# RWKV preparation and inversion: key norms summed token-major, sigmoids of both directions together, triangular inversion by predicated copies without GpSimd

## The chip, the cores and the metric

One core of one Trainium2 chip runs the whole program. The metric is the device time in microseconds (us) of one execution, and the median of several runs counts. Engines are called PE (TensorE), DVE (VectorE), ACT (ScalarE), POOL (GpSimd) and SP (SyncE, which here only issues transfers).

## The reference

The program computes two trunk layers over 384 tokens (128 of a prompt, 256 latent ones, width 1024). Each layer is a SwiGLU half step, a token mixer and another SwiGLU half step, each with adaptive modulation and a layer norm behind it. The mixer has three branches: differential attention, gated linear attention (GLA) and RWKV-7. The change touches the RWKV branch (and a clamp inside the GLA stage):

```python
kk = heads(k * lp['rw_k_k'])
kk = kk / jnp.maximum(jnp.sqrt(jnp.sum(jnp.square(kk), -1, keepdims=True)), 1e-12)
for d, pd in enumerate((dir_f, dir_b)):
    w_raw = lp['rw_w0'][d] + jnp.tanh(wd) @ lp['rw_w_up'][d]
    decay = jnp.exp(-jnp.exp(-jax.nn.softplus(-w_raw) - 0.5))
    a = jax.nn.sigmoid(lp['rw_a0'][d] + ad @ lp['rw_a_up'][d])
    kd = heads(k * (1.0 + (a - 1.0) * lp['rw_k_a']))
    ...
    y, s_fin = rwkv7_scan(*seq, s0[:, d])
```

With four heads of 64 and chunks of 64 tokens, `rwkv7_scan` is done chunk-wise: prefix sums of the log decay (a scan along the tokens), decayed keys and receptances, 64x64 products of them, the inverse X of a unit triangular 64x64 matrix per chunk, head and direction, and then products with that inverse.

## The kernel before

A layer is one block of straight code per engine; the stages are separated by `meet()`, a meeting of PE, DVE, ACT and POOL. SP streams the weights, 1 MB at a time, into a ring of six slots, and a slot is refilled when PE releases it (`used`). While attention, GLA and RWKV run, the ring is full and nothing is fetched. Feature-major tiles have features on the 128 partitions and tokens along the row: `WIN` is the stretch of 385 columns that holds three groups of 128 tokens, and a `wide` tile is two such rows (770 columns, four heads).

**GLA tail** (DVE `gla()`, lines 2063 to 2087). Behind the last GLA output DVE scales the keys (L2068), squares them (L2070), and works on the GLA outputs. In between it takes the sums of squares, which PE makes with a 128x128 block of ones so that each sum stands on all 64 partitions of its head (L1114, 2 x 385 columns), and clamps them (L2079). ACT takes the root of the 770 columns (L1670).

**Preparation** (`rwkv()` of each engine). DVE inverts the 770 roots (L2091) and normalises the keys (L2092). Then, for direction 0 and after it direction 1: PE's low-rank products `lora(d)` (L1104), four sigmoids on ACT into `sw` (decay) and `sa` (rate) (L1663, L1665), two scans on DVE (L2101) and a subtraction (L2103), three exponentials on ACT (L1680, L1683, L1684), the keys on DVE (L2108, L2111), four products on DVE (L2114 to L2118) and three small copies (L2121). `sw`, `sa` and `cs` exist once, so `rates(1)` waits for `decay_used`, at the end of direction 0. POOL makes `be = sa * kk` (L2343) and `rkd = r * kn` (L2347) for each direction; the second `rkd` waits for PE's bonus product of the first (`bonus_mm`), and the bonus product (L1135) is what DVE copies last (L2125) before the meeting. PE does `products(0)` and `products(1)` (L1083) behind `decay_used` of direction 0.

**Units** (`rwkv_units()`, lines 1139 on for PE, 2127 on for DVE). Six (group, direction) products are masked into SBUF by DVE, `masked(n)` (L2133 and L2135, two of each per n); ACT copies the raw products into `am` (L1691), and `first(g)` masks them (L2143). The inverse is made level by level for three groups: X0 is the inverse so far, X1 its transpose, and at each of the levels v = 1 to 5 the off-diagonal half L of `am` gives X0 <- X0 - X0 L X0. PE forms L X0 (L1168) for three groups, ACT copies it (L1698), PE forms X0 L X0 (L1179) and its transpose (L1186), and DVE subtracts them from the banks (L2163, L2168). POOL adds the identity to both halves of each group (L2357, six times 128x512) and masks `am` for each level into `off` (L2361); PE waits for `off_ready` before each L1168. Behind it come token-major copies, the solves (L1209) with a negation on DVE (L2181), and the carries.

Of the kernel before, what the change touches and what calls it, by code (L numbers as in the profile page):

```python
# [9 lines left out]
I32 = mybir.dt.int32  # L10
# [96 lines left out]
def shape_constants():  # L107
# [102 lines left out]
def trunk_kernel(nc, x_in, c_in, consts, weights, w_ad, par_in, ln_in, row_in, bgate_in, rw_state_in, gla_state_in,  # L210
                 kc_in, vc_in, first_ada, b_first, y_out, rw_out, gla_out, k_out, v_out, dumps=None):
    with ExitStack() as ctx:
# [35 lines left out]
        arena, arena_r = with_rounded("arena", [P, 23660])  # L248
# [87 lines left out]
        g_kl = put(2 * TOK).rearrange("p (d t) -> p d t", d=2)  # L336
        g_o = put(2 * GROUPS * GLA_W).rearrange("p (d g n) -> p d g n", d=2, g=GROUPS)
        g_st = lnrow[:, 0, :].rearrange("p (d s n) -> p d s n", d=2, s=2)
# [22 lines left out]
        put.at = 0  # L361
        sw, sa, cs = wide(), wide(), wide()
        assert put.at <= ffn_mark
# [23 lines left out]
        off = by_head()  # L387
# [37 lines left out]
        att_sum = small[:, 28:52].rearrange("p (u c) -> p u c", c=2)  # L425
        diff_ss = small[:, 52:64]
# [107 lines left out]
        norm_root = sem("norm_root")  # L534
        kk_ready = sem("kk_ready")
# [9 lines left out]
        decay_used = sem("decay_used")  # L545
        bonus_in = sem("bonus_in")
# [5 lines left out]
        xz_first = sem("xz_first")  # L552
        xz_ready = sem("xz_ready")
        off_ready = sem("off_ready")
# [218 lines left out]
        def layer(l, last):  # L773
            with nc.Block() as block:
# [29 lines left out]
                def _(pe):  # L804
# [293 lines left out]
                    def rwkv():  # L1098
# [14 lines left out]
                        for i in range(2):  # L1113
                            mm = pe.matmul(ps[4 + i][:, 0:WPAD - 2], con("ones_blk"), kk[:, i, WIN], start=True, stop=True)  # L1114
# [9 lines left out]
                        lora(1)  # L1124

# [13 lines left out]
                    def rwkv_units():  # L1139
# [285 lines left out]
                def _(sc):  # L1425
# [230 lines left out]
                    def rwkv():  # L1656
                        def rates(d):
                            sc.wait_ge(lora_mm, d + 1)
                            if d == 1:
                                sc.wait_ge(decay_used, 1)  # L1660
                                sc.wait_ge(rate_kk, 1)
                            for i in range(2):
                                sc.activation(sw[:, i, WIN], ps[4 * d + 2 * i][:, 0:WPAD - 2], ACT.Sigmoid,  # L1663
                                              bias=w0[:, d, i:i + 1])
                                ins = sc.activation(sa[:, i, WIN], ps[4 * d + 2 * i + 1][:, 0:WPAD - 2], ACT.Sigmoid,  # L1665
# [4 lines left out]
                        sc.activation(pp[:, :, WIN], pp[:, :, WIN], ACT.Sqrt).then_inc(norm_root, 1)  # L1670
# [4 lines left out]
                        ins.then_inc(values_out, 1)  # L1675
                        for d in range(2):
                            if d == 1:
                                rates(1)
                            sc.wait_ge(cum_ready, d + 1)
# [104 lines left out]
                def _(ve):  # L1784
# [175 lines left out]
                    def gla():  # L1960
# [128 lines left out]
                    def rwkv():  # L2089
                        ve.wait_ge(norm_root, 1)  # L2090
                        own.link(ve.reciprocal(pp[:, :, WIN], pp[:, :, WIN]))  # L2091
                        ve.tensor_tensor(kk[:, :, WIN], kn[:, :, WIN], pp[:, :, WIN], ALU.mult).then_inc(kk_ready, 1)  # L2092
                        ve.wait_ge(kk_ready, 1)
                        k_, r_ = psh[:, 4:6, WIN], psh[:, 2:4, WIN]
                        for d in range(2):
                            ve.wait_ge(rates_ready, d + 1)
                            for i in range(2):
                                a, b, keep = cs[:, i, WIN], sw[:, i, WIN], rw_keep[:, d, WIN]
# [4 lines left out]
                            ve.tensor_tensor(sw[:, :, WIN], cs[:, :, WIN], sw[:, :, WIN], ALU.subtract).then_inc(cum_ready, 1)  # L2103

                            if d == 1:
# [410 lines left out]
```

## Time and profile before

| | |
|---|---|
| median of three runs | 2249.46 us (2248.36 to 2250.56) |
| profiled execution | 2254.03 us |
| its span, first to last instruction | 2252.2 us |
| mean granted TensorE clock | 0.917 of full speed |
| busy PE / DVE / ACT / POOL | 1960.7 / 1091.1 / 703.3 / 120.1 us |
| layer 2: GLA tail and preparation | 1719.8 to 1765.8 us |
| layer 2: units up to the first X0 L X0 | 1765.8 to 1784.2 us |
| layer 2: rest of the inversion | 1784.2 to 1821.6 us |

Times inside a trace are from the start of the span. Layer 1 passes through the same stages 1109.3 us earlier. A row of the chain or the timeline gives start and duration; "x32" means that many instructions in a row, and an instruction that follows another without a wait overlaps it by its latency, so that the distance of two starts is less than a duration. A multiplication of full 32-bit numbers stands as two PE records. Where a program's row names `arena`, it is the one large SBUF tensor out of which nearly all tiles are cut.

### The profile page before, as it was taken

To read this page: it belongs to the slowest core of one execution; us is meant where nothing else is said; L and a number is where in the kernel's file an instruction comes from. 1 tells how busy PE (TensorE), PEld (TensorE's weight loads), DVE (VectorE), ACT (ScalarE), POOL (GpSimd) and SP (SyncE) were. 2 spreads that over 40 slices of the span, in tenths; PEclk is the share of its full clock that TensorE was granted. 3 is DMA by queue.
4 is the path that set the end of the run, shared out by engine and by line. 5 is a ranking of instruction groups with operands and counts; after the bars stand their busy time and mean duration, and the time that the engine had idled before them with its cause. 6 is when DMAs were issued, how large, how long until landed. Compare 5 with 4: busy or idle time off the path is not lost. (4 is left out here: it accounts for less than half of the span.)

```text
span 2252.2 us, 36981 instructions
## 1 busy us (share of the span) xinstructions
PE 1960.7 (87%) x15584; PEld 1727.6 (77%) x15584; DVE 1091.1 (48%) x1655; ACT 703.3 (31%) x1155; POOL 120.1 (5%) x104
## 2 busy tenths in 40 slices
PE   5999998997549779999969999999964688899995
PEld 3899995985439659999849999869843686699994
DVE  0434336526674663343453343454287647634345
ACT  1422222335432332222232222133354223422221
POOL 1000001000031010000010000010000400100000
PEclk9899998998669989999969999989976799899998
DMA  7533336331000173333463333453300003633320
GB/s 321 219 131 130 116 127 261 113 125 53 13 1 4 60 280 112 131 125 118 152 241 133 129 130 116 156 214 132 122 23 8 2 4 112 257 120 130 130 93 28
DMA packets 40402, 274.39 MB, mean 122 GB/s; under 512 B 4740, under 2 KB 6548, under 8 KB 8288
## 3 DMA queue, kind: packets, MB, share of 16 engines
q1 hardware_dynamic: 35280, 255.34, 32.1%
q0 software_dynamic: 2400, 11.50, 1.3%
q10 hardware_dynamic: 2608, 5.88, 0.7%
q8 instruction: 90, 1.47, 0.3%
q14 instruction: 24, 0.20, 0.0%
HBM read 269.29 MB, written 3.41 MB: 121 GB/s over the span
## 5 line engine op out<-in xcount | busy, mean ns | idle before, releaser
L1791 DVE TENSOR_TENSOR ring_r<-ring,arena_r 128x1024 fp32r<-128x1024 f32 x280 | 327.6, 1221 | 657.7 <-ACT arena_r L1433 657.5
L842 PE MATMUL bank<-arena_r,ring_r 128*128 128x384 f32 x1728 | 586.9, 340 | 0.0
L838 PE MATMUL bank<-arena_r 128*128 128x384 f32 (+1 forms) x1504 | 519.0, 345 | 18.7 <-DVE arena_r L1811 12.9
L841 PE MATMUL bank<-arena_r 128*128 128x384 f32 x1408 | 475.7, 338 | 0.0
L842 PEld LDWEIGHTS bank<-arena_r,ring_r 128*128 128x128 f32 x1728 | 327.2, 189 | 0.0
L838 PEld LDWEIGHTS bank<-arena_r 128*128 128x128 f32 x1504 | 286.6, 191 | 30.8 <-DVE ring_r L1791 18.2
L884 PE MATMUL bank<-arena_r 128*128 128x512 f32 x1056 | 300.7, 393 | 0.0
L1433 ACT ACTIVATE arena_r<-ring 128x1024 fp32r<-128x1024 f32 x280 | 276.7, 1050 | 42.0 <-PE bank L842 30.4
L1472 ACT ACTIVATE arena<-bank 128x384 f32<-128x384 f32 x88 | 43.3, 492 | 756.9 <-PE bank L842 756.9
L841 PEld LDWEIGHTS bank<-arena_r 128*128 128x128 f32 x1408 | 265.7, 189 | 4.7 <-issue 1.0
L884 PEld LDWEIGHTS bank<-arena_r 128*128 128x128 f32 x1056 | 197.3, 188 | 38.5
L884 PE MATMUL bank<-ring_r,arena_r 128*128 128x512 f32 x528 | 164.4, 392 | 0.0
L666 PE MATMUL bank<-ring,silu_c 128*32 128x256 f32 x1152 | 101.3, 498 | 50.3 <-DVE arena L1847 29.2
L1791 DVE TENSOR_TENSOR ring_r<-ring,lnrow_r 128x1024 fp32r<-128x1024 f32 x60 | 73.4, 1225 | 147.3 <-ACT lnrow_r L1433 147.2
L884 PEld LDWEIGHTS bank<-ring_r,arena_r 128*128 128x128 f32 x528 | 99.1, 188 | 23.0
L838 PE MATMUL bank<-arena_r,lnrow_r 128*128 128x384 f32 x320 | 111.5, 349 | 4.0 <-DVE ring_r L1791 4.0
L666 PEld LDWEIGHTS bank<-ring,silu_c 128*32 128x32 f32 x1152 | 39.3, 135 | 97.4 <-DVE arena L1847 31.6
L841 PE MATMUL bank<-arena_r,lnrow_r 128*128 128x384 f32 x320 | 107.9, 337 | 0.0
L1433 ACT ACTIVATE lnrow_r<-ring 128x1024 fp32r<-128x1024 f32 x60 | 63.3, 1059 | 142.5 <-PE bank L842 142.5
L2324 POOL TENSOR_TENSOR x<-x,lnrow 128x1024 f32<-128x1024 f32 x12 | 28.2, 2348 | 1359.5 <-DVE x L1870 1359.5
L841 PE MATMUL bank<-ring_r,arena_r 128*128 128x512 f32 (+1 forms) x240 | 89.8, 374 | 0.0
L838 PEld LDWEIGHTS bank<-arena_r,lnrow_r 128*128 128x128 f32 x320 | 60.7, 190 | 5.9 <-DVE ring_r L1791 5.4
(295 smaller groups left out, 2372.1 us busy)
## 6 DMA issues: line engine op xcount, KB each, us to landing
ring<-weights SPq DMA_DIRECT2D x230, 1024.0 KB, 4.9
ring<-first_ada SPq DMA_DIRECT2D x12, 1024.0 KB, 13.4
lnrow<-ln_in POOLq DMA_DIRECT2D x6, 1024.0 KB, 6.5
const<-consts ACTq DMA_DIRECT2D x1, 2403.0 KB, 12.5
x<-x_in ACTq DMA_DIRECT2D x1, 1536.0 KB, 18.3
y_out<-x SPq DMA_DIRECT2D x3, 512.0 KB, 2.6
rows<-row_in POOLq DMA_DIRECT2D x2, 736.0 KB, 14.2
par<-par_in POOLq DMA_DIRECT2D x2, 626.0 KB, 8.8
```

The source lines that it names most:

```text
L666: mm = pe.matmul(ps[q // 2][rows_at, (q % 2) * 256:(q % 2) * 256 + 256], silu_c[:, 2 * (k % 2):2 * (k % 2) + 32], ring_tile(n0 + q)[:, k, ...
L838: mm = pe.matmul(out, w_h, h_h, start=start, stop=False, skip_group_check=True)
L841: pe.matmul(out, w_h, h_l, start=False, stop=False, skip_group_check=True)
L842: return pe.matmul(out, w_l, h_h, start=False, stop=stop, skip_group_check=True)
L884: mm = pe.matmul(ps[2 + 2 * g + n][:, :], a, w[:, n * 512:n * 512 + 512], start=(first and a is a_hi and w is hi), stop=(last and a is a_l ...
L1433: sc.activation(place, unit_of(FIRST[stretch], u), ACT.Copy).then_inc(w_rounded, 1)
L1472: sc.activation(sgt[:, b, :], ps[0][:, 0:TOK], ACT.Silu).then_inc(silu_done, 1)
L1791: ve.tensor_tensor(low_unit(FIRST[stretch], u), raw, place.bitcast(F32), ALU.subtract).then_inc(w_ready, 1)
L2324: po.tensor_tensor(x[:, g, :], x[:, g, :], lnrow[:, 1, :], ALU.add).then_inc(x_ready, 1)
```

## The change

1. **Norms.** PE multiplies each 128x128 tile of squares (now the stationary operand) by two columns of the block of ones, into 12 columns of one bank: the sums stand with tokens on partitions. Clamp, root and inverse act on 128x12. Twelve products of the inverse (one column stepped by zero into 64) with the identity then spread them back over the 64 partitions of each head, into banks 0 and 1, behind `lora(1)`; DVE multiplies out of PSUM.
2. **Order.** `sw`, `sa` and `cs` exist for both directions (`sw[1]` and `sa[1]` in parts of `psh` that are dead by then; `g_o` moves to the arena's start and the arena grows by 44 columns). ACT does both sets of sigmoids, then all exponentials. DVE does scan 0, kk, keys 0, scan 1, products 0, keys 1, products 1. The first product waits for the first exponential alone.
3. **Inversion.** ACT writes minus the identity into all of X0 and X1 ahead of time (two copies of 128x1536, behind the exponentials of direction 0), so the tiles hold minus the inverse. DVE puts the masked values in with `copy_predicated`, in place of the multiplications by a mask and the subtractions; PE uses the whole `am` and the mask of the level decides which of the results are written. POOL's part of the units, `off` and six semaphore waits go. The negation L2181 becomes a plain copy.

```diff
 # constants
-    first[:, 0, d] = -1.0 * half(cs, ct, 1, 1 - d)
-    first[:, 1, d] = -1.0 * half(cs, ct, 1, d)
+    first[:, 0, d] = half(cs, ct, 1, 1 - d)
+    first[:, 1, d] = half(cs, ct, 1, d)
 # tiles
-sw, sa, cs = wide(), wide(), wide()
+sw, sa, cs = (wide(), psh[:, 6:8, :]), (wide(), psh[:, 8:10, :]), (wide(), wide())
+kk_norm = small[:, 28:40]
 # PE, rwkv
-for i in range(2):
-    mm = pe.matmul(ps[4 + i][:, 0:WPAD - 2], con("ones_blk"), kk[:, i, WIN], start=True, stop=True)
+for g in range(GROUPS):
+    for i in range(2):
+        mm = pe.matmul(ps[4][:, 4 * g + 2 * i:4 * g + 2 * i + 2], kk[:, i, pcol(g):pcol(g) + P],
+                       con("ones_blk")[:, 0::64], start=True, stop=True)
 mm.then_inc(norm_mm, 1)
...
 lora(1)
+pe.wait_ge(norm_inv, 1)
+pe.wait_ge(rates_ready, 1)
+for i in range(2):
+    for g in range(GROUPS):
+        o, width = pcol(g) - 1, P + 1 if g == 0 else P
+        for par in range(2):
+            n = 4 * g + 2 * i + par
+            mm = pe.matmul(ps[i][64 * par:64 * par + 64, o:o + width],
+                           kk_norm[:, n:n + 1].to_broadcast([P, 64]), const[:, 0:width],
+                           start=True, stop=True)
+mm.then_inc(norm_wide, 1)
 # PE, units
-pe.wait_ge(off_ready, n + 1)
 if v == 1:
-    pe.wait_ge(xz_ready, 2 * g + 1)
-    if g == 1:
-        pe.wait_ge(prod_ready, 5)
-    else:
-        pe.wait_ge(am_ready, 2 if g == 0 else 3)
+    pe.wait_ge(prod_ready, (3, 5, 6)[g])
+    pe.wait_ge(am_ready, (2, 2, 3)[g])
...
-        mm = pe.matmul(ps[LX_BANK[g]][k, o:o + 64], off[k, g, d, h, :], xz[k, 0, g, d, h, :],
+        mm = pe.matmul(ps[LX_BANK[g]][k, o:o + 64], am[k, g, d, h, :], xz[k, 0, g, d, h, :],
                        start=True, stop=True)
...
-    pe.wait_ge(xz_ready, 2 * g + 2)
+    pe.wait_ge(xz_ready, g + 1)
 # ACT, rwkv
     sc.wait_ge(lora_mm, d + 1)
-    if d == 1:
-        sc.wait_ge(decay_used, 1)
-        sc.wait_ge(rate_kk, 1)
...
-sc.activation(pp[:, :, WIN], pp[:, :, WIN], ACT.Sqrt).then_inc(norm_root, 1)
+sc.activation(kk_norm, kk_norm, ACT.Sqrt).then_inc(norm_root, 1)
...
+rates(1)
 for d in range(2):
-    if d == 1:
-        rates(1)
     sc.wait_ge(cum_ready, d + 1)
-    own.link(sc.activation(sw[:, :, WIN], sw[:, :, WIN], ACT.Exp, scale=DECAY))
-    if d == 0:
-        sc.wait_ge(kk_ready, 1)
-    own.link(sc.activation(pp[:, :, WIN], cs[:, :, WIN], ACT.Exp, scale=DECAY))
-    sc.activation(cs[:, :, WIN], cs[:, :, WIN], ACT.Exp, scale=-DECAY).then_inc(decay_exp, 1)
+    ins = sc.activation(sw[d][:, :, WIN], sw[d][:, :, WIN], ACT.Exp, scale=DECAY)
+    ins.then_inc(decay_first, 1)
+    if d == 1:
+        sc.wait_ge(decay_used, 1)
+    own.link(sc.activation(pp[:, :, WIN], cs[d][:, :, WIN], ACT.Exp, scale=DECAY))
+    sc.activation(cs[d][:, :, WIN], cs[d][:, :, WIN], ACT.Exp, scale=-DECAY).then_inc(decay_exp, 1)
+    if d == 0:
+        for s in range(2):
+            sc.activation(xz[:, s, :, :, :, :].rearrange("p g d h n -> p (g d h) n"),
+                          ident64.unsqueeze(1).to_broadcast([P, 2 * GROUPS * HEADS, CHUNK]), ACT.Copy,
+                          scale=-1.0).then_inc(xz_filled, 1)
 # DVE, gla
-for i in range(2):
-    ins = ve.tensor_scalar(pp[:, i, WIN], ps[4 + i][:, 0:WPAD - 2], 1e-24, None, ALU.max)
-ins.then_inc(norm_sq, 1)
+ve.tensor_scalar(kk_norm, ps[4][:, 0:12], 1e-24, None, ALU.max).then_inc(norm_sq, 1)
 # DVE, rwkv: cumulate(d) is L2096 to L2103, keys(d) L2107 to L2112, decayed(d) L2114 to L2122
-own.link(ve.reciprocal(pp[:, :, WIN], pp[:, :, WIN]))
-ve.tensor_tensor(kk[:, :, WIN], kn[:, :, WIN], pp[:, :, WIN], ALU.mult).then_inc(kk_ready, 1)
+    def decayed(d):
+        ve.wait_ge(decay_first, d + 1)
+        own.step(ve.tensor_tensor(kr[:, 0, d, :, WIN], kk[:, :, WIN], sw[d][:, :, WIN], ALU.mult))
         ve.wait_ge(decay_exp, d + 1)
...
+ve.reciprocal(kk_norm, kk_norm).then_inc(norm_inv, 1)
+cumulate(0)
+ve.wait_ge(norm_wide, 1)
+for i in range(2):
+    ins = ve.tensor_tensor(kk[:, i, WIN], kn[:, i, WIN], ps[i][:, 0:WPAD - 2], ALU.mult)
+ins.then_inc(kk_ready, 1)
+ve.wait_ge(kk_ready, 1)
+keys(0)
+cumulate(1)
+decayed(0)
+ve.wait_ge(decay_used, 1)
+ve.wait_ge(bonus_in, 1)
+keys(1)
+decayed(1)
 # DVE, units
-        ins = ve.tensor_tensor(xz[:, 0, g, d, par::2, :], got[:, :, 0, :],
-                               rw_first[:, 0, d, :].unsqueeze(1).to_broadcast([P, 2, CHUNK]), ALU.mult)
+        ins = ve.copy_predicated(
+            xz[:, 0, g, d, par::2, :],
+            rw_first[:, 0, d, :].bitcast(I32).unsqueeze(1).to_broadcast([P, 2, CHUNK]), got[:, :, 0, :])
...
-    ve.tensor_tensor(xz[:, 1, g, :, :, :], am[:, g, :, :, :],
-                     rw_first[:, 1, :, :].unsqueeze(2).to_broadcast(wide), ALU.mult).then_inc(xz_first, 1)
+    ve.copy_predicated(xz[:, 1, g, :, :, :],
+                       rw_first[:, 1, :, :].bitcast(I32).unsqueeze(2).to_broadcast(wide),
+                       am[:, g, :, :, :]).then_inc(xz_ready, 1)
+ve.wait_ge(xz_filled, 2)
 masked(0)
...
-if v == 1:
-    ve.wait_ge(xz_ready, 2 * g + 2)
-else:
-    ve.wait_ge(inv_ready, n - GROUPS + 1)
 ve.wait_ge(xlx0_mm, n + 1)
-ins = ve.tensor_tensor(xz[:, 0, g, :, :, :].rearrange("p d h n -> p (d h n)"),
-                       xz[:, 0, g, :, :, :].rearrange("p d h n -> p (d h n)"),
-                       ps[XLX_BANK[g]][:, :], ALU.subtract)
+ins = ve.copy_predicated(
+    xz[:, 0, g, :, :, :], rw_halves[:, ::-1, v - 1, :].bitcast(I32).unsqueeze(2).to_broadcast(wide),
+    ps[XLX_BANK[g]][:, :].rearrange("p (d h n) -> p d h n", d=2, h=HEADS))
...
-    ve.tensor_scalar(to[:, g, :, :, :].rearrange("p d h n -> p (d h n)"), ps[bank][:, :], -1.0, None,
-                     ALU.mult).then_inc(uw_out, 1)
+    ve.tensor_copy(to[:, g, :, :, :].rearrange("p d h n -> p (d h n)"),
+                   ps[bank][:, :]).then_inc(uw_out, 1)
 # POOL: be reads sa[d]; rwkv_units (L2349 to L2363) is gone
```

## Rows read from the trace of the kernel before

**Rows 1.** The page: busy time of the engines.

```profile
PE 1960.7 (87%) x15584; PEld 1727.6 (77%) x15584; DVE 1091.1 (48%) x1655; ACT 703.3 (31%) x1155; POOL 120.1 (5%) x104
```

**Rows 2.** Windows: length, busy PE, PEld, DVE, ACT, POOL, granted clock, DMA share, GB/s.

```profile
1719.80:1765.81 46.01, 14.62 (x114) 10.62 (x114) 40.06 (x44) 20.13 (x26) 9.19 (x6) 0.65 0.03 9
1765.81:1784.20 18.39, 12.82 (x324) 12.36 (x326) 11.76 (x27) 3.17 (x8) 13.47 (x11) 0.69 0.01 2
1784.20:1821.63 37.43, 37.36 (x1250) 37.12 (x1248) 17.88 (x26) 7.76 (x13) 10.71 (x11) 0.99 0.02 4
610.46:656.48 46.02, 14.62 (x114) 10.62 (x115) 40.04 (x44) 20.15 (x26) 9.18 (x6) 0.65 0.03 9
...
1778.70:1784.20 5.50, 3.94 (x68) 3.75 (x70) 0.00 (x0) 0.60 (x1) 5.50 (x5) 0.50 0.00 0
```

**Rows 3.** Chain that ended last, layer 2: start, us, what.

```profile
1733.17 4.98 DVE arena L2091
...
1739.17 3.13 DVE arena L2101 x2
...
1746.03 1.74 DVE arena L2114
...
1750.66 1.28 ACT L1663
...
1753.99 3.13 DVE arena L2101 x2
...
1770.72 2.51 POOL arena L2357 x2
...
1782.23 1.97 PE bank L1168 x32
...
1785.55 0.93 PE bank L1186 x32
```

**Rows 4.** Timeline of DVE: preparation.

```profile
1744.10 0.96 DVE L2111 TENSOR_TENSOR arena<-arena 128x770 f32<-128x770 f32 x1
...
1747.69 0.95 DVE L2115 TENSOR_TENSOR arena<-arena 128x770 f32<-128x770 f32 x1
```

**Rows 5.** Timeline of all engines: start, us, engine, line, form.

```profile
1721.08 1.49 ACT L1650 ACTIVATE arena<-arena 128x1536 f32<-128x1536 f32 x1
...
1725.54 1.02 DVE L2079 TENSOR_SCALAR arena<-bank 128x385 f32<-128x385 f32 x2
1725.66 0.22 ACT L1654 ACTIVATE small<-small 128x24 f32<-128x24 f32 x1 [1.80 <-DVE small L2076]
...
1731.66 2.94 PE L1104 MATMUL bank<-arena,par 64*128 64x385 f32 x8 [5.73 <-issue]
...
1750.65 3.69 PE L1083 MATMUL bank<-arena 64*64 64x128 f32 x64 [16.05 <-DVE arena L2121]
...
1754.28 1.50 PE L1135 MATMUL bank<-par,arena 128*128 128x4 f32 x12
...
1767.25 0.55 DVE L2133 TENSOR_TENSOR arena<-bank,const 128x384 f32<-128x384 f32 x1
...
1767.72 0.28 DVE L2135 TENSOR_TENSOR arena<-bank,const 128x128 f32<-128x128 f32 x1
...
1773.62 0.66 ACT L1691 ACTIVATE arena<-bank 128x256 f32<-128x256 f32 x2 [1.69 <-PE bank L1094]
```

**Rows 6.** Single lines: count, shortest/median/longest ns, first and last start.

```profile
L2101 DVE TENSOR_TENSOR_SCAN arena<-const,arena x8: 959/1600/2243, 629.8 to 1754.9; 128x385 f32<-128x385 f32 x8
...
L2343 POOL TENSOR_TENSOR arena<-arena x4: 2178/2218/2259, 630.0 to 1754.0; 128x770 f32<-128x770 f32 x4
...
L2347 POOL TENSOR_TENSOR arena<-arena x4: 1812/1813/1814, 635.8 to 1760.0; 128x770 f32<-128x770 f32 x4
...
L2015 DVE COPY_PREDICATED arena<-const,bank x32: 561/571/585, 577.4 to 1699.6; 128x384 f32<-128x384 int32 x32
...
L2163 DVE TENSOR_TENSOR arena<-arena,bank x30: 686/687/689, 676.3 to 1821.7; 128x512 f32<-128x512 f32 x30
```

More of the change, by code:

```diff
@@ L247, in trunk_kernel @@
         small = sb("small", [P, 192])
-        arena, arena_r = with_rounded("arena", [P, 23660])
+        arena, arena_r = with_rounded("arena", [P, 23704])
         def con(name):
@@ L336, in trunk_kernel @@
         g_kl = put(2 * TOK).rearrange("p (d t) -> p d t", d=2)
+        g_st = lnrow[:, 0, :].rearrange("p (d s n) -> p d s n", d=2, s=2)
+        put.at = 0
         g_o = put(2 * GROUPS * GLA_W).rearrange("p (d g n) -> p d g n", d=2, g=GROUPS)
-        g_st = lnrow[:, 0, :].rearrange("p (d s n) -> p d s n", d=2, s=2)
         put.at = 0
@@ L386, in trunk_kernel @@
         am = by_head()
-        off = by_head()
         assert put.at <= ffn_mark + 10 * WPAD
@@ L534, in trunk_kernel @@
         norm_root = sem("norm_root")
+        norm_inv = sem("norm_inv")
+        norm_wide = sem("norm_wide")
         kk_ready = sem("kk_ready")
@@ L545, in trunk_kernel @@
         decay_used = sem("decay_used")
+        decay_first = sem("decay_first")
         bonus_in = sem("bonus_in")
@@ L551, in trunk_kernel @@
         am_ready = sem("am_ready")
-        xz_first = sem("xz_first")
+        xz_filled = sem("xz_filled")
         xz_ready = sem("xz_ready")
-        off_ready = sem("off_ready")
         lx_mm = sem("lx_mm")
@@ L1658, in rates @@
                             sc.wait_ge(lora_mm, d + 1)
-                            if d == 1:
-                                sc.wait_ge(decay_used, 1)
-                                sc.wait_ge(rate_kk, 1)
                             for i in range(2):
-                                sc.activation(sw[:, i, WIN], ps[4 * d + 2 * i][:, 0:WPAD - 2], ACT.Sigmoid,
+                                sc.activation(sw[d][:, i, WIN], ps[4 * d + 2 * i][:, 0:WPAD - 2], ACT.Sigmoid,
                                               bias=w0[:, d, i:i + 1])
-                                ins = sc.activation(sa[:, i, WIN], ps[4 * d + 2 * i + 1][:, 0:WPAD - 2], ACT.Sigmoid,
+                                ins = sc.activation(sa[d][:, i, WIN], ps[4 * d + 2 * i + 1][:, 0:WPAD - 2], ACT.Sigmoid,
                                                     bias=a0[:, d, i:i + 1])
@@ L2089, in rwkv, with cumulate @@
                     def rwkv():
-                        ve.wait_ge(norm_root, 1)
-                        own.link(ve.reciprocal(pp[:, :, WIN], pp[:, :, WIN]))
-                        ve.tensor_tensor(kk[:, :, WIN], kn[:, :, WIN], pp[:, :, WIN], ALU.mult).then_inc(kk_ready, 1)
-                        ve.wait_ge(kk_ready, 1)
-                        k_, r_ = psh[:, 4:6, WIN], psh[:, 2:4, WIN]
-                        for d in range(2):
+                        def cumulate(d):
                             ve.wait_ge(rates_ready, d + 1)
                             for i in range(2):
-                                a, b, keep = cs[:, i, WIN], sw[:, i, WIN], rw_keep[:, d, WIN]
+                                a, b, keep = cs[d][:, i, WIN], sw[d][:, i, WIN], rw_keep[:, d, WIN]
                                 if d == 1:
@@ L2102, in rwkv, with keys @@
                             own.settle()
-                            ve.tensor_tensor(sw[:, :, WIN], cs[:, :, WIN], sw[:, :, WIN], ALU.subtract).then_inc(cum_ready, 1)
-                            if d == 1:
-                                ve.wait_ge(bonus_in, 1)
+                            ve.tensor_tensor(sw[d][:, :, WIN], cs[d][:, :, WIN], sw[d][:, :, WIN],
+                                             ALU.subtract).then_inc(cum_ready, 1)
+                        def keys(d):
                             for i in range(2):
-                                own.step(ve.tensor_scalar(kn[:, i, WIN], sa[:, i, WIN], prm("k_a")[:, i:i + 1], ka1[:, i:i + 1],
-                                                          ALU.mult, ALU.add))
+                                own.step(ve.tensor_scalar(kn[:, i, WIN], sa[d][:, i, WIN], prm("k_a")[:, i:i + 1],
+                                                          ka1[:, i:i + 1], ALU.mult, ALU.add))
@@ L2347, in rwkv @@
                             po.tensor_tensor(rkd[:, :, WIN], psh[:, 2:4, WIN], kn[:, :, WIN], ALU.mult).then_inc(bonus_in, 1)
-                    def rwkv_units():
-                        wide = [P, 2, HEADS, CHUNK]
-                        for v in range(1, RW_LEVELS):
-                            for g in range(GROUPS):
-                                if v == 1:
-                                    po.wait_ge(xz_first, g + 1)
-                                    for s in range(2):
-                                        half = xz[:, s, g, :, :, :].rearrange("p d h n -> p (d h) n")
-                                        po.tensor_tensor(half, half, ident64.unsqueeze(1).to_broadcast([P, 2 * HEADS, CHUNK]),
-                                                         ALU.add).then_inc(xz_ready, 1)
-                                else:
-                                    po.wait_ge(lx_mm, GROUPS * (v - 2) + g + 1)
-                                po.tensor_tensor(off[:, g, :, :, :], am[:, g, :, :, :],
-                                                 rw_halves[:, :, v - 1, :].unsqueeze(2).to_broadcast(wide),
-                                                 ALU.mult).then_inc(off_ready, 1)
                     po.dma_start(par[:, :], par_in[l]).then_inc(par_loaded, 16)
```

23 lines of the change are left out of this document (10 added, 13 removed).

## The prediction

> **What bounds the kernel now.** The page says that PE is busy for 87% of the span [rows 1], which hides where it is not. I cut the mixer of layer 2 by stage. The GLA tail and the preparation take 46.0 us with PE busy for 14.6 and DVE for 40.1: a DVE chain. The first part of the units takes 18.4 us with DVE at 11.8 and POOL at 13.5: a mixed chain. The rest of the inversion takes 37.4 us with PE busy for 37.4: PE alone. DMA is at 0.01 to 0.03 in all three, so no transfer waits, and layer 1 repeats the stage to 0.01 us [rows 2]. Whatever leaves the chain comes off the time once per layer, since the ring is full and both engines and transfers start again behind the mixer.
>
> The chain of waits then names the pieces [rows 3]: an inverse of 770 columns, 4.98 us; two scans, 3.13 us, twice; an ACT table load at 1750.66, from which four sigmoids lead to the second pair of scans at 1753.99; POOL's identity additions from 1770.72; PE's last L1168, 1.97 us, before X0 L X0 begins at 1784.20.
>
> One thing in it is not what it seems. A scan of 385 columns takes 0.96 us when alone and 2.24 when second, and POOL's `be` beside it 2.2 us where the same shape takes 1.81 elsewhere [rows 6]. Likewise the first product, 1.74 us in the chain [rows 3], where its neighbour of the same shape takes 0.95 [rows 4]. So DVE operations with two SBUF inputs stand still while POOL runs. The Trainium skill says this of the pair of SBUF ports that both engines use (SBUF — State Buffer, Who interferes with whom): whoever starts first holds it for the whole instruction. By that rule the trace agrees (2.24 for 0.96).
>
> **Part 1, norms.** Clamping 12 columns in place of 2 x 385 (1.02 us from 1725.54) lets the next operation start when ACT has the GLA roots, at about 1725.95 [rows 5] instead of 1726.5: 0.5 us. The inverse falls from 4.98 us to about 0.2. The six products for the norms have 12 records like L1135 (1.5 us), the same as PE spent before, and DVE comes for them later anyway: nothing.
>
> The spread is new: 24 records of 128 columns with 128x64 weights, a form that the trace doesn't show. It starts when `lora(1)` ends. That began at 1731.66 and took 2.94 us; the shorter clamp and root bring ACT forward by 1.2 us, so it ends at 1733.4. Priced per column like those 8 records of 385 columns, 24 take 2.9 us; like L1083 (0.058 us a record) 1.4 [rows 5]; with no two halves in parallel twice the first, 5.9. I take L1104's price, being nearest in size: the end is near 1736.2. The Trainium skill (TensorEngine Tiling (Array Packing), Key Properties) says that tiles of one mode run in parallel and that a change of mode drains PE first; the first would give the 2.9, the second adds a drain behind `lora(1)` that no row prices.
>
> **Part 2, order.** I lay DVE's new sequence out on layer 2's clock, from 1732.65 (0.5 before the old inverse). With 770 columns a product takes 0.97 with its wait and 0.87 in a row [rows 4].
> - Inverse to 1732.9; two scans without POOL, 1.8, to 1734.7; subtraction to 1735.7. Wait for the spread and its latency: 0.4, to 1736.1.
> - kk out of PSUM in two halves, 1.0: 1737.1. Now POOL starts `be`, 1.81 us. Keys take 1.9 and their last product stands behind POOL for 0.9: 1739.9.
> - Second pair of scans beside POOL's `rkd`, 3.1 as now: 1743.0. POOL goes straight on to the second `be`; the subtraction waits some 1.4: 1745.4.
> - Four products and three copies, 3.85 (0.87 more than from 1747.69 to PE's start at 1750.65 [rows 4, 5]): 1749.25. Keys 1: 1751.15. Products 1: 1755.0.
> - But DVE isn't last now. `products(0)` and `(1)` on PE take 3.7 behind 1749.25, the first bonus product 1.5 [rows 5]: 1754.5. Only then may POOL do the second `rkd`, 2.0 with a little blocking: 1756.5. The second bonus product takes 1.5 at the high clock and up to 3.0 at the low; I take 2.1, then copies and meeting: 1759.0.
>
> Against 1765.8 that is 6.8 us. ACT is no limit: sigmoids from 1733.4 (2.05, which is 3.33 less the load of 1.28 [rows 3]), a load, three exponentials, then the two fills of 1536 columns at 1.49 each like L1650 [rows 5], done by 1742.3, while the next prefix sum comes at 1745.4. If that cover went, a fill twice as dear would still fit. The serial sigmoids of direction 1 with their load are what vanish; what is late next is the bonus chain.
>
> **Part 3, inversion.** DVE's sequence in old times: from 1765.9 six masked products at 2 x (0.47 + 0.20) = 1.33 [rows 5], with two 512-column copies between, 0.62 each: 1775.1. `copy_predicated` out of PSUM is in the trace: 0.57 us for 384 columns, where the multiplication takes 0.55 [rows 5, 6]. Out of SBUF it isn't shown; I take the same rate, with twice as the other end. PE: ACT reads the last raw product at 1773.6 [rows 5], so L1168 runs at 0.93 for each of three groups behind that and all three end at 1776.4, where X0 L X0 starts. It started at 1784.20: 7.8 us. Before, PE had fallen to a granted 0.50 (1.2 GHz) from 1778.7 to 1784.2 [rows 2], and the first L1179 still took 1.35 (to 1785.55 [rows 3]) instead of 0.93; without the gaps, 0.4 more.
>
> The rest stays PE's: nine groups of 0.93, 8.4 us a level, against six copies of about 0.62 in place of six subtractions of 0.69 [rows 6]. Dropping `off` saves nothing there (PE never waited in 37.4 us), the plain copy for the negation nothing. Sum of part 3: 8.2.
>
> **Sum.** 6.8 + 8.2 = 15.0 us a layer, 30.0 in all: 2254.0 of the profiled execution becomes 2224.0, and the median, 4.6 below it, 2249.5 becomes **2219.5**.
>
> **Rivals.**
> 1. *Spread and ports cost more* (0.17): the spread unpacked at the low clock ends 3.1 later, and the scaling in keys (one tensor, two numbers), if it too stands behind POOL, adds 0.9. 4.0 a layer: 2227.5. For: PE comes out of an idle stretch. Against: `lora(1)` precedes it. The Trainium skill (SBUF — State Buffer, Who interferes with whom) counts such single-input operations in a two-port mode among the contenders.
> 2. *POOL doesn't get in the way* (0.11): DVE wins each race, or POOL's work falls into ACT waits; then 0.9, 1.4 and the 1.3 in the scans come back, and the bonus product at the high clock 0.6: 4.2 a layer, 2211.
> 3. *The clock* (0.06): PE is at the low level through one level of the inversion, nine groups at 1.97 in place of 0.93 [rows 3], about 9 us a layer: 2238. For: the granted clock falls in the preparation, 0.65 on average [rows 2]. Against: PE is busy from the meeting on.
> 4. *Nothing arrives* (0.03): what was saved is waited for behind the mixer, 2245 to 2249. The DMA share of 0.02 speaks against it.
> 5. *Slower* (0.03): predicated copies with a broadcast mask run far below the rate of L2015. From 1.4 us per 512 columns on, six of them exceed PE's 8.4 and DVE sets each level. Four levels at 6c - 8.4, and the equal of five more copies at c - 0.62, eat the 15.0 at c = 1.8 us; at c = 2.0 the time is 2262. Against: L2015 has a broadcast mask and PSUM source too and runs at full rate [rows 6].
>
> **How the numbers follow.** The forecast has 0.60. All dear ends of case 1 with copies at twice the rate (3.1) would give about 2234, all cheap ones 2211; I reach from 2211 to 2232, leaving out most of 3, 4 and 5. A measurement of this kernel tells 0.2%, 4.5 us, from no change. Faster: 0.60 + 0.17 + 0.11 + 0.06 = 0.94; same 0.03; slower 0.03.
>
> **What would show it.** Preparation from the last GLA output to the meeting near 39 us (46.0 now); the first L1179 some 10.5 us behind the meeting (18.4); the level at 8.4 us; copies of 512 columns at 0.7 us; one table load fewer ahead of the second scans; PE's idle time before the second bonus product ending with POOL's `rkd`; a second scan still at 2.2 and a subtraction near 2.3. I am wrong if the wait for the spread passes 1 us, if DVE rather than PE bounds a level, or if the granted clock in the first level is 0.50.

## The result and the profile after

The changed kernel takes 2218.2 us, median of four runs, against 2248.9 us beside it: a ratio of 0.9863, 95% interval 0.9833 to 0.9893. Two further measurements of the same code gave 0.9875 [0.9858, 0.9893] and 0.9866 [0.9843, 0.9888]. The mean of the three, 0.9868, is 29.7 us of 2249.5; 2219.5 and 30.0 us were forecast.

The page's line of busy times, against [rows 1]:

```profile
PE 1954.8 (88%) x15648; PEld 1726.1 (78%) x15648; DVE 1079.5 (49%) x1655; ACT 702.6 (32%) x1155; POOL 73.1 (3%) x62
```

The profiled execution took 2217.1 us with a span of 2215.3. POOL has lost 42 instructions and 47 us. PE is 5.9 us less busy and DVE 11.6, so the greater part of what was saved is their idle time. The windows of layer 2, against [rows 2]: from 0.3 us ahead of the GLA tail to the meeting's end, to the first X0 L X0, to the end of the inversion. Columns: stretch, its length, busy time and instructions of PE, PEld, DVE, ACT, POOL, granted clock, DMA share, GB/s.

```profile
1697.90:1739.45 41.55, 20.93 (x150) 16.52 (x154) 34.90 (x44) 19.76 (x27) 9.93 (x6) 0.55 0.03 10
1739.45:1749.79 10.34, 9.94 (x320) 9.66 (x322) 9.93 (x27) 3.18 (x8) 0.00 (x0) 0.81 0.01 4
1749.79:1786.80 37.01, 36.94 (x1254) 36.64 (x1250) 19.05 (x26) 7.77 (x13) 0.00 (x0) 1.00 0.02 4
```

Measured in every trace between the same two instructions, the first operation of the GLA tail and the first masked product, the preparation was 46.1 us and is 41.25. From there to the first X0 L X0 it was 18.1 and is 10.33. Each figure repeats within 0.1 us from layer to layer and from trace to trace. The rest of the inversion was 37.6 to 38.6 us in the four instances at hand with the old inversion (mean 38.0) and is 36.5 in 18 of 22 with the new one (37.0 here, 37.9 at most; mean 36.6). Per layer 4.85 + 7.75 + 1.4 = 14.0, so 28 of the 29.7 us lie where the change is. The two first traces differ by 36.9 us; what is above 30 is within the scatter, since before alone ran from 2238.8 to 2257.4 us over these measurements.

DVE, POOL and PE in the new preparation, from the timeline of layer 2 (start, duration, engine, line, form; brackets: idle time before it and what ended it), against [rows 3 to 5]:

```profile
1711.04 0.23 DVE L2133 RECIPROCAL small<-small 128x12 f32<-128x12 f32 x1
1711.18 1.75 DVE L2106 TENSOR_TENSOR_SCAN arena<-const,arena 128x385 f32<-128x385 f32 x2
1711.92 1.84 PE L1135 MATMUL bank<-const,small 128*64 128x129 f32 x24
...
1713.84 1.01 DVE L2137 TENSOR_TENSOR arena<-arena,bank 128x385 f32<-128x385 f32 x2
...
1714.89 2.37 DVE L2113 TENSOR_SCALAR arena<-arena,par,small 128x385 f32<-128x385 f32 x2
1715.01 2.03 POOL L2366 TENSOR_TENSOR arena<-arena 128x770 f32<-128x770 f32 x1 [15.39 <-DVE arena L2137]
...
1718.30 3.39 DVE L2106 TENSOR_TENSOR_SCAN arena<-const,arena 128x385 f32<-128x385 f32 x2
1718.34 2.53 POOL L2370 TENSOR_TENSOR arena<-arena 128x770 f32<-128x770 f32 x1 [1.30 <-DVE arena L2116]
1720.83 2.45 POOL L2366 TENSOR_TENSOR arena<-arena 128x770 f32<-128x770 f32 x1
1721.72 2.38 DVE L2108 TENSOR_TENSOR arena<-arena 128x770 f32<-128x770 f32 x1
...
1727.87 3.69 PE L1084 MATMUL bank<-arena 64*64 64x128 f32 x64 [14.11 <-DVE arena L2129]
...
1731.48 2.72 PE L1149 MATMUL bank<-par,arena 128*128 128x4 f32 x12
...
1734.35 1.81 POOL L2370 TENSOR_TENSOR arena<-arena 128x770 f32<-128x770 f32 x1 [11.07 <-PE bank L1149]
...
1736.22 2.72 PE L1149 MATMUL bank<-par,arena 128*128 128x4 f32 x12 [2.01 <-POOL arena L2370]
```

The inverse of 4.98 us is 0.23, and the spread is done when DVE comes for it. Every DVE operation that runs beside POOL is long: 2.37 for a pair that takes 0.87 alone, 3.39 for 1.75, 2.38 for 0.96. DVE's last copies of the preparation (L2129) end at 1733.5, but the meeting waits until 1739.3 for the chain at the foot: first bonus product, POOL's `rkd`, second bonus product.

The new units of the inversion, from the view of single lines (count, shortest/median/longest ns):

```profile
L2159 DVE COPY_PREDICATED arena<-const,bank x24: 292/296/301, 651.0 to 1748.5; 128x128 f32<-128x128 int32 x24
...
L2168 DVE COPY_PREDICATED arena<-const,arena x6: 736/742/749, 654.5 to 1748.7; 128x512 f32<-128x512 int32 x6
...
L2186 DVE COPY_PREDICATED arena<-const,bank x30: 725/731/735, 662.0 to 1786.9; 128x512 f32<-128x512 int32 x30
```

A predicated copy of 512 columns takes 0.73 us out of PSUM and 0.74 out of SBUF, against 0.69 for the subtraction it replaces [rows 6].

### The profile page after: what moved, and what is told of

Its sections match the earlier page's. It is cut to its first block and busy times, and to the rows that moved or that the text cites. A ratio compares the mean times of both kernels' runs of the same rounds, so it can differ in the third digit from the quotient of the medians.

```text
span 2215.3 us, 37011 instructions
## 1 busy us (share of the span) xinstructions
PE 1954.8 (88%) x15648; PEld 1726.1 (78%) x15648; DVE 1079.5 (49%) x1655; ACT 702.6 (32%) x1155; POOL 73.1 (3%) x62
## 3 DMA queue, kind: packets, MB, share of 16 engines
q8 instruction: 90, 1.47, 0.3%
## 5 line engine op out<-in xcount | busy, mean ns | idle before, releaser
L839 PE MATMUL bank<-arena_r 128*128 128x384 f32 (+1 forms) x1504 | 520.0, 346 | 17.8 <-DVE arena_r L1823 12.9
L885 PEld LDWEIGHTS bank<-arena_r 128*128 128x128 f32 x1056 | 197.3, 188 | 38.5
L667 PEld LDWEIGHTS bank<-ring,silu_c 128*32 128x32 f32 x1152 | 38.5, 133 | 96.1 <-DVE arena L1859 31.6
## 6 DMA issues: line engine op xcount, KB each, us to landing
const<-consts ACTq DMA_DIRECT2D x1, 2403.0 KB, 12.9
rows<-row_in POOLq DMA_DIRECT2D x2, 736.0 KB, 14.2
```

The source lines that it names most:

```text
L667: mm = pe.matmul(ps[q // 2][rows_at, (q % 2) * 256:(q % 2) * 256 + 256], silu_c[:, 2 * (k % 2):2 * (k % 2) + 32], ring_tile(n0 + q)[:, k, ...
L839: mm = pe.matmul(out, w_h, h_h, start=start, stop=False, skip_group_check=True)
L885: mm = pe.matmul(ps[2 + 2 * g + n][:, :], a, w[:, n * 512:n * 512 + 512], start=(first and a is a_hi and w is hi), stop=(last and a is a_l ...
```

## The experiments

The theory: inversion and preparation add up, the inversion is what was forecast, and the preparation ends with the bonus chain, slow through POOL's turn in it and through PE's clock; DVE's long operations are waits for POOL. Diffs are against the changed kernel. "Preparation", "first X0 L X0" and "rest" are the three stretches defined above; both layers agree within 0.1 us in the first two, unless two numbers stand.

**1. The parts apart.** The changed kernel again, and one with the preparation as changed and the inversion as before.

```diff
-    first[:, 0, d] = half(cs, ct, 1, 1 - d)
+    first[:, 0, d] = -1.0 * half(cs, ct, 1, 1 - d)
...
-    ins = ve.copy_predicated(xz[:, 0, ...], rw_halves[...], ps[XLX_BANK[g]][...])
+    ins = ve.tensor_tensor(xz[:, 0, ...], xz[:, 0, ...], ps[XLX_BANK[g]][:, :], ALU.subtract)
...
+    po.tensor_tensor(half, half, ident64..., ALU.add).then_inc(xz_ready, 1)
+    po.tensor_tensor(off[:, g, ...], am[:, g, ...], rw_halves[...], ALU.mult).then_inc(off_ready, 1)
```

> The changed kernel itself, once more, beside the three that follow. Theory (the stage times of the two traces add up): 13.1 us a layer from the preparation (4.9, at 41.1 us) and the first part of the units (7.7, at 10.5 us), so 26 us in all against the kernel before, 0.988 of it; whatever else two single traces differ by (some 10 us) is chance of the clock and the start. Rival (the rest is part of the change too, by a clock that stays up): 36 us, 0.984.

> Preparation as changed, inversion as before (POOL adds the identity and masks off). Theory (the two parts add up): the preparation still takes 41.1 us a layer, 4.9 less than before, the first part of the units 18.2 as before, so about 10 us less than before (2239). Rival (the parts share a cause, as the clock or the position in time): the preparation alone gives under 5 us or over 20.

The whole change: 0.9875, stages 41.2, 10.3, 36.5. Preparation alone: 2241.8 us, 0.9963 [0.9947, 0.9978], stages 41.2, 18.1, 37.6 and 38.6. The two parts don't touch each other: each stage has the length that its own code gives it, and the preparation is worth 4.9 us a layer, 9.8 in all; the ratio says 8.3 (5 to 12).

**2. The bonus chain.** The first bonus product is issued ahead of the products of direction 0, not behind them.

```diff
-    pe.wait_ge(decay_used, 1)
-    products(0)
-    products(1)
     for d in range(2):
         pe.wait_ge(bonus_in, d + 1)
...
+        if d == 0:
+            pe.wait_ge(decay_used, 1)
+            products(0)
+            products(1)
```

> The changed kernel, but PE does the bonus product of direction 0 as soon as its input is there, ahead of the two products that wait for the end of direction 0. Theory (the bonus chain behind DVE's last product sets the meeting: 3.7 of products, 2.7, POOL 1.8, 2.7): POOL's second rkd comes right behind keys 1 and DVE, which is done 5.8 us ahead of the meeting, becomes the last but for a second bonus product; the preparation falls from 41.1 to 36 to 37 us, so 8 to 10 us less than the changed kernel in all (2209). It may cost 0.9 where the second rkd now stands beside DVE's last four products. Rival (the meeting waits for something else, as ACT or the cost of a meeting): still 41 us.

2215.4 us, 0.985 [0.9832, 0.9868]; preparation 37.5 us, 3.8 less per layer. Its timeline:

```profile
1719.10 2.69 PE L1145 MATMUL bank<-par,arena 128*128 128x4 f32 x12 [7.27 <-POOL arena L2370]
...
1727.89 2.60 POOL L2370 TENSOR_TENSOR arena<-arena 128x770 f32<-128x770 f32 x1 [6.50 <-DVE arena L2116]
1728.72 2.58 DVE L2123 TENSOR_TENSOR arena<-arena 128x770 f32<-128x770 f32 x1
1730.54 2.72 PE L1145 MATMUL bank<-par,arena 128*128 128x4 f32 x12 [0.89 <-POOL arena L2370]
1732.97 0.30 DVE L2129 COPY arena<-arena 128x4 f32<-128x4 f32 x3
```

The product itself is as slow as before, but it lies in PE's idle time, and POOL's second `rkd` now follows DVE's keys at once. It meets a DVE product there and holds it up by 1.6 us. DVE and the bonus chain end together, near 1733.3.

**3. The order alone.** The serial order of directions is put back; norms and inversion stay.

```diff
 keys(0)
-cumulate(1)
 decayed(0)
+cumulate(1)
...
-rates(1)
 for d in range(2):
+    if d == 1:
+        rates(1)
```

In `rates(1)` ACT waits for the products of direction 0 again, as before.

> The changed kernel, but with the order of the kernel before: sigmoids, scan and keys of direction 1 only behind the products of direction 0 (with their two table loads). Norms and inversion stay as changed. Theory (what the new order wins on DVE is waited for again behind the bonus chain, and the norms alone give the 4.9): the preparation takes 40 to 42 us, as the changed one does with 41.1, and the time is the same within 2 us. Rival (the order is worth what I summed for it, the sigmoids and the load off the chain, some 3 us a layer): 44 us, 6 us slower.

2223.6 us, 0.9879 [0.9862, 0.9897]; preparation 41.15 us, against 41.25. As the change stands, the new order gives nothing. In the serial order DVE waits for the second sigmoids, but the first bonus product is issued early enough to hide beside the second scans; in the new order DVE is done earlier and the bonus chain is late. With experiment 2's move on top the new order takes 37.5. The serial order with that move was not run; in its trace DVE's own chain ends with the meeting, so the move should give little there.

**4. The norms alone.** The norms as before (sum over 128 rows, 770 columns clamped, rooted, inverted); order and inversion stay.

```diff
-    pe.matmul(ps[4][:, 4 * g + 2 * i:...], kk[:, i, ...], con("ones_blk")[:, 0::64], ...)
+    pe.matmul(ps[4 + i][:, 0:WPAD - 2], con("ones_blk"), kk[:, i, WIN], ...)
...
-    ve.reciprocal(kk_norm, kk_norm).then_inc(norm_inv, 1)
+    own.link(ve.reciprocal(pp[:, :, WIN], pp[:, :, WIN]))
```

> The changed kernel with the norms as before (the sum spread over 128 rows by the product, 770 columns clamped, rooted and inverted), order and inversion as changed. Theory (the norms are worth the 0.5 of the clamp and the 4.75 of the inverse, since both stand in DVE's chain ahead of everything in the preparation, and the spread is covered by the first scans): preparation from the GLA tail to the meeting 46.0 to 46.8 us per layer, against 41.25 with all three parts; some 10.5 us slower than the whole change, ratio to the kernel before 0.991 to 0.993. The serial order undone alone gave 41.15, so order and norms would then account for the 4.9 as nothing and all. Rival (with the long inverse the new order hides something of it, since the sigmoids of both directions run beside it): 43 to 44.5 us. First XLX 10.3 us behind the meeting in both.

2232.8 us, 0.9933 [0.991, 0.9957]; preparation 45.5 us, 4.2 more than with the new norms, where 4.8 to 5.5 was expected. The missing part is in PE:

```profile
1716.33 4.96 DVE L2122 RECIPROCAL arena<-arena 128x770 f32<-128x770 f32 x1
...
1738.01 3.56 PE L1082 MATMUL bank<-arena 64*64 64x128 f32 x64 [20.25 <-DVE arena L2118]
...
1741.49 1.50 PE L1134 MATMUL bank<-par,arena 128*128 128x4 f32 x12
...
1743.38 1.92 DVE L2118 COPY arena<-arena 128x4 f32<-128x4 f32 x3
```

Counted from the GLA tail's start (1702.96), the products of direction 0 start at 35.05 us here and at 29.66 in the changed kernel: 5.4 later, more than the whole inverse. But the first bonus product takes 1.50 and not 2.72, its stretch having a granted clock of 1.00 instead of 0.50. What the chain loses, the clock partly gives back. The last line belongs to experiment 5: the three small copies that take 0.30 us elsewhere stand beside POOL's second `rkd` (1743.14, 1.99 us) here.

**5. POOL and DVE.** POOL's product `be` is made twice.

```diff
+    own.link(po.tensor_tensor(be[:, d, :, WIN], sa[d][:, :, WIN], kk[:, :, WIN], ALU.mult))
     po.tensor_tensor(be[:, d, :, WIN], sa[d][:, :, WIN], kk[:, :, WIN], ALU.mult).then_inc(rate_kk, 1)
```

> POOL's product be is computed twice, one behind the other, in both directions; the result is the same. Theory (DVE stands still while POOL's instruction runs): the pair of scalings behind be(0) goes from 2.4 to about 4.2, or the operation behind it does, and the subtraction behind be(1) from 2.4 to about 4.2; preparation 1.5 to 3.6 us longer than 41.25 per layer, most of it in DVE's own durations. Rival (only the first DVE operation behind a start is delayed, or the delay isn't POOL's): durations within 0.2 of the changed kernel's, preparation 41.3.

2231.9 us (one run); preparation 44.35 us, 3.1 more. The operation that stands beside the added product is each time the one that grew:

```profile
1726.09 2.37 DVE L2113 TENSOR_SCALAR arena<-arena,par,small 128x385 f32<-128x385 f32 x2
...
1728.31 1.81 POOL L2368 TENSOR_TENSOR arena<-arena 128x770 f32<-128x770 f32 x1
1728.49 2.46 DVE L2116 TENSOR_TENSOR arena<-arena 128x770 f32<-128x770 f32 x1
...
1736.04 2.41 POOL L2368 TENSOR_TENSOR arena<-arena 128x770 f32<-128x770 f32 x1
1736.70 2.56 DVE L2121 TENSOR_TENSOR arena<-arena 128x770 f32<-128x770 f32 x1
```

0.96 became 2.46 and 0.95 became 2.56, 3.1 in all and exactly the stage's loss. Then the opposite: `be` and `rkd` on DVE, no product on POOL, and the first bonus product ahead.

```diff
-    po.tensor_tensor(be[:, d, ...], ...).then_inc(rate_kk, 1)
...
-    po.tensor_tensor(rkd[:, :, WIN], ...).then_inc(bonus_in, 1)
...
+    ve.tensor_tensor(rkd[:, :, WIN], psh[:, 2:4, WIN], kn[:, :, WIN], ALU.mult).then_inc(bonus_in, 1)
...
+    ve.tensor_tensor(be[:, d, :, WIN], sa[d][:, :, WIN], kk[:, :, WIN], ALU.mult).then_inc(rate_kk, 1)
```

> No arithmetic of the preparation on POOL: both be and both rkd products go to DVE, and the first bonus product stands ahead of the products of direction 0. Theory (POOL's four operations hold the SBUF port against DVE and cost more than they save): the two k_a scalings take 0.9 together where they took 2.4, the second pair of scans 1.8 where it took 3.4, the second subtraction 0.96 where it took 2.4, and rkd of direction 1 no longer delays its neighbour by 1.7; against these 6.0 us stand four products of 0.87, 3.5, and a little settling: preparation 34.5 to 35.5 us per layer against 37.5 with the bonus product first alone and 41.25 in the changed kernel. Time 2204 to 2210 beside a kernel before of 2249, ratio 0.981 to 0.983. Rival (POOL's work was parallel and DVE's losses are its own, the operations simply slow there): the times of scans and scalings stay as they are, 3.5 is added: 41 us, ratio 0.988.

2210.2 us, 0.9835 [0.9811, 0.9858]; preparation 34.8 us, within the 34.5 to 35.5 expected.

```profile
1715.43 0.86 DVE L2113 TENSOR_SCALAR arena<-arena,par,small 128x385 f32<-128x385 f32 x2
...
1718.20 1.80 DVE L2106 TENSOR_TENSOR_SCAN arena<-const,arena 128x385 f32<-128x385 f32 x2
1718.43 2.69 PE L1145 MATMUL bank<-par,arena 128*128 128x4 f32 x12 [5.48 <-DVE arena L2120]
1720.04 0.96 DVE L2108 TENSOR_TENSOR arena<-arena 128x770 f32<-128x770 f32 x1
```

The three long operations are back at 0.86, 1.80 and 0.96. DVE does four more products and is done earlier. Once more, beside the changed kernel on the same chip:

> The kernel with all arithmetic of the preparation on DVE and the first bonus product ahead, once more, beside the changed kernel on the same chip. Theory (6.4 us per layer, 12.9 in all): ratio to the kernel before 0.9805 to 0.983, 12 to 14 us below the changed kernel. Rival (the rest of the program gives back part of it, through the clock or the waits behind the meeting): 5 to 10 us below the changed kernel.

> The changed kernel once more, as the partner of the one before: ratio to the kernel before 0.9865 to 0.988 on the two earlier measurements of 0.9863 and 0.9875.

2209.9 us, 0.9819 [0.9803, 0.9834], against 2222.6 us, 0.9866 [0.9843, 0.9888]: 12.7 us, where the stages say 12.9. It beats both kernels.

**6. The clock.** 40 products of 128x128 into an unused bank on PE, behind the spread and ahead of `products(0)`; their result is not used. Then 58 of them.

```diff
+    pe.wait_ge(rates_ready, 2)
+    for _ in range(40):
+        pe.matmul(ps[6][:, 0:P], ident, ident, start=True, stop=True)
     pe.wait_ge(decay_used, 1)
     products(0)
```

> 40 products of 128x128 into an unused bank, on PE behind the spread and ahead of the products of direction 0, in the stretch in which PE was idle for 14 us; their result is not used. Theory (the two bonus products at 2.7 us each and the 64 products at 3.7 us are slow through the granted clock, which is low behind the idle stretch): the 64 products of direction 0 go to 2.0 to 2.4 us, the first bonus product to 1.5, the second, behind another idle stretch of 2 us, to 1.5 to 2.7: preparation 38 to 39.5 us per layer against 41.25, ratio 0.984. Rival (these products are bound by something else, for instance by their small sizes, 4 columns each): durations unchanged, 41.3; a third way is that the 40 products are not done when DVE's first results are there, then longer than 41.3.

> As the kernel with 40 unused products, but 58 of them: 40 took 9.2 us and ended 4.6 us ahead of the products of direction 0, which then ran at the low clock as before (3.69 us). Theory (the clock falls in that last idle stretch of 4.6 us; with PE busy until 0.5 to 1 us before them it stays up): the 18 more take 3.9 us, the 64 products of direction 0 go from 3.69 to about 2.0, the first bonus product to 1.5, the second, behind 2 us of idling, to 1.5 to 2.7: preparation 37 to 39.5 us per layer against 41.25. Rival (these products are bound by something else than the granted clock): 3.7, 2.7, 2.7 us again and 41.3.

With 40: 2224.9 us, 0.9893 [0.9872, 0.9914]; preparation 41.3 us, nothing gained. They took 9.2 us at a granted 1.00 and ended 4.6 us too early; behind that gap the clock was 0.50 again, with 3.69 and 2.72 us. So this run tells nothing on the theory, and the longer one decides by its stage: preparation 38.4 us, 2.9 less. Its time, 2220.1 us, is one run and within the scatter.

```profile
1717.04 13.22 PE L1141 MATMUL bank<-const 128*128 128x128 f32 x116 [0.17 <-ACT arena L1675]
...
1731.46 1.99 PE L1084 MATMUL bank<-arena 64*64 64x128 f32 x64 [1.20 <-DVE arena L2132]
1733.38 1.50 PE L1152 MATMUL bank<-par,arena 128*128 128x4 f32 x12
...
1736.90 2.72 PE L1152 MATMUL bank<-par,arena 128*128 128x4 f32 x12 [2.02 <-POOL arena L2373]
```

The 58 products are 116 records. The same 64 products of direction 0 take 1.99 instead of 3.69 and the first bonus product 1.50 instead of 2.72: 2.9 together, the gain. The second, behind 2 us of idling, stays at 2.72.

**7. The price of the copies.** Each predicated copy of the inversion is made twice; one of the four places is shown.

```diff
+    own.link(ve.copy_predicated(xz[:, 0, g, ...], rw_halves[...], ps[XLX_BANK[g]][...]))
     ins = ve.copy_predicated(xz[:, 0, g, ...], rw_halves[...], ps[XLX_BANK[g]][...])
```

> Every predicated copy of the inversion is made twice, so that one costs DVE some 0.5 (128 columns) and 1.5 us (512 columns); the result is the same. Theory (up to the first X0 L X0 the inversion is DVE's sequence: six masked products with their copies and two 512-column copies; in the levels it is PE's at 8.4 us, so that DVE only decides from 1.4 us a copy): first X0 L X0 13.0 to 14.2 us behind the meeting, against 10.33; six copies at 1.5 are 9.2 us a level, 0.8 above PE, so the rest of the inversion goes from 36.5 to 38.5 to 40.5. Rival (PE sets the first X0 L X0 too, and DVE has room in the levels): 10.3 to 11 and 36.5 again. A second rival (each copy of a level stands in the path between PE's groups, since a group waits for its own copy): 8 times 0.7 or more, over 42.

2256.4 us (one run); first X0 L X0 after 16.7 and 15.9 us, rest 47.7 and 45.0. Both are above what the theory expected (13.0 to 14.2, 38.5 to 40.5), for three reasons. Ahead of the first X0 L X0 there are twelve copies of 128 columns, not the six I counted: 12 x 0.33 and 2 x 0.74 make 5.4, and 10.3 + 5.4 = 15.7. In the levels the timeline of layer 2 shows one whole level:

```profile
1779.68 1.10 PE L1189 MATMUL bank<-lnrow,arena 64*64 64x64 f32 x32
...
1780.83 0.73 DVE L2192 COPY_PREDICATED arena<-const,bank 128x512 f32<-128x512 int32 x1 [0.77 <-PE bank L1189]
...
1788.47 0.72 DVE L2203 COPY_PREDICATED arena<-const,bank 128x512 f32<-128x512 int32 x1
1789.24 1.15 PE L1178 MATMUL bank<-arena 64*64 64x64 f32 x32 [1.59 <-DVE arena L2203]
1790.23 1.10 PE L1189 MATMUL bank<-lnrow,arena 64*64 64x64 f32 x32
```

A level is a loop: 1.15 us until the first copy may start, 8.4 of copies (1780.83 to 1789.24), 1.0 for the last group's L1178; 10.55 in all, 2.15 above PE's 8.4, and four such levels give 8.6 us, where layer 2 lost 8.5. By this estimate DVE decides from 6c + 2.15 = 8.4, so from c = 1.04 us a copy, and not from 1.4. The third reason is PE's clock in layer 1: granted 0.50 from about 665 to 671 and from 689 to 692, where layer 2 had 1.00. The last L1178 took 1.97 us there, not 1.15, and the rest 2.7 us more. The second rival's number (over 42) came true, but not its mechanism: inside the level PE goes from group to group, and its one long wait, 1.59 us, is for the level's last copy.

## Why the prediction was right, and where it was not

**Where the kernel was bound.** Right: idle PE behind a DVE chain, and a mixed chain behind the meeting. What left them came off the time, 28 of 29.7 us.

**Part 1, norms.** Nearly right. Inverse 0.23 us for 0.2. The spread takes 1.84 us, between 1.4 and the 2.9 chosen; it ends at 1713.76 and DVE starts behind it at 1713.84 without a wait, where 0.4 us had been set aside. By experiment 4 the norms shorten DVE's chain by 5.4 us, and 4.2 arrive. The norm products were priced at 1.5 us; they took 2.69 in some instances and 1.47 in others, without a trace of it in the 41.25.

**Part 2, DVE's schedule.** Right in sum: from the reciprocal to the last copy 22.35 us were laid out and 22.5 ran. Two errors of 0.6 us cancel in it: DVE came to kk sooner, and keys took 3.4 us from 1714.89 to 1718.30, not 2.8. The wait for POOL fell on the scaling (a pair 2.37, not 0.87) and not on the product behind it (0.96). That is the second half of rival 1, its mechanism true and its price 0.6 instead of 0.9. The Trainium skill (SBUF — State Buffer, Who interferes with whom) names operations with two SBUF inputs and single-input ones in a two-port mode as those that wait for POOL; the trace agrees for the scans (1.6 us). The scaling, with one tensor, waits too (1.5 us); whether it runs in such a mode no run here tells.

**Part 2, the bonus chain.** The failed term: bonus products at 1.5 and 2.1 us measured 2.72 each. That is 1.8 of the 2.05 us between 39.2 and 41.25. The prediction had named this chain as the last to end. Its 1.5 us came from a row: in the kernel before, the same two groups took 3.69 and then 1.50 us [rows 5], the bonus product at a granted 1.00, in both layers. In the changed kernel they take 3.69 and 2.72, the clock at 0.50 through both, and so they do in all 16 instances that have the spread and the old place of the bonus product, the 58 unused products of experiment 6 aside; in experiment 4, without the spread, it is 1.50 again. Why the clock rises between the two groups in one kernel and not in the other no run tells. The 2.1 us for the second was a middle between 1.5 and 3.0, though the kernel before has that product too (1761.83 on PE): 2.72 us. Experiment 6 shows that these times are the clock's. That the order of directions gives nothing as it stands (experiment 3) was not forecast: it was booked as part of the 6.8, while it only moved the wait from ACT's sigmoids to the bonus chain.

**Part 3.** The size was right: 7.75 us for 7.8. The bound was not quite: three groups of the product ahead of it (L1168, now L1178) were laid on PE behind ACT's last read. In the chain of the changed kernel, below, this stretch is DVE's unit by unit, and only one such group (L1178) stands behind its last masked product; start, us, what:

```profile
1748.10 0.45 DVE arena L2157
1748.55 0.22 DVE arena L2159
1748.81 1.15 PE bank L1178 x32
1749.96 0.93 PE bank L1189 x32
```

Where the 7.75 us lay, the timeline of the kernel before says: PE waited 1.24, 2.81 and 1.52 us for POOL ahead of the three L1168, and two of them took 1.97 us where the first took 1.15. That makes 7.2; no run takes the pieces of this part apart.

In the rest of the inversion 0.4 us was booked for PE's slow start and 1.4 came. The first two groups (X0 L X0 and its transpose) take 1.87 us at 1.00; in the four instances with the old inversion they took 2.33, 2.32, 2.99 and 3.17, at a granted 0.50 to begin with. So the slow start is worth 0.8 on average: 0.5 in the trace that the prediction had, up to 1.3 in the other. The remaining 0.6 is open. It lies in single groups that take a few tenths longer at a granted 1.00, and these occur with the new inversion too (0.5 us in the trace above, 1.4 at most).

**The rivals.** 2 (POOL not in the way) was wrong in the trace, and experiment 5 shows what it is worth when it is made true. 3 (clock in a level): 1.00 in the inversion of the changed kernel; experiment 7's layer 1 shows that it can happen, at 2.7 us in the rest. 4 fell by the stages. 5: a copy takes 0.73 us; experiment 7 shows the mechanism and moves its threshold from 1.4 to 1.04 us, so by that estimate the levels would have cost 4 x 4.55 at 1.8, not 4 x 2.4.

**The time.** That 2219.5 came within 1.3 us of 2218.2 is luck, for the steps were not as close: 2.0 us a layer too much was forecast to be saved in the preparation and 1.0 too little in the rest of the inversion, by the stages 2 us in all, and the interval of the first measurement alone is 6.7 us to either side.

## What to carry to other kernels

Draw the new chain for every engine of a meeting, not only for the one that was last before: here DVE was done 5.8 us ahead of a chain of two small products and one POOL product, and moving one of them in PE's queue gave 3.8 us a layer. A price read from a row carries that row's clock with it: the same two groups behind idle time took 3.69 and 1.50 us in one kernel, 3.69 and 2.72 in the other. So lay out such a product at both levels and let the dearer one into the sum. Work given to POOL is not free where DVE is the bound and both read SBUF: here four products on DVE cost 3.5 us and returned 6 us of DVE's own waits.

## What the runs showed of the hardware that was not expected

- `tensor_scalar` on 385 fp32 columns with its two scalars in SBUF waits for POOL like an operation with two inputs: 0.87 us a pair alone, 2.37 beside POOL's product (experiment 5, both ways). Plain copies wait as well: three of 128x4 took 0.30 us alone and 1.92 beside POOL's product (experiment 4).
- POOL's product, too, gets longer when it starts just behind a DVE operation: 1.81 us alone, 2.03 to 2.60 in those cases.
- Unused products kept PE's clock up only where the next work followed closely: with 4.6 us between them and the products of direction 0 it was 0.50 again, with 1.2 us it was 1.00. The second bonus product of the same run, behind 2 us without work, ran at 0.50.
- The same two groups of PE products, behind an idle stretch of 14 to 16 us each time, met a different clock: the second ran at 1.00 (1.50 us) in the kernel before and at 0.50 (2.72 us) in the changed one, in both layers.
